# Products of three fp32r matmuls on split operands become one plain fp32 matmul

## Chip, cores and metric

The program runs on one core of one Trainium2 chip. The metric is the device time of one execution in microseconds (us). Tensors are fp32 in memory.

## What is computed

Two blocks over 256 latent tokens ("x") and 256 context tokens, of width 1024, each of two layers. Cut to what matters:

```python
# first block, per layer l (context tokens only where a later layer needs them)
hx = rms_norm(x, norm1_g[l]) * (1.0 + sc1) + sh1
y_lat, y_ctx = token_mixers(hx, hc, w_in[l], w_out[l], ...)  # gating, Fourier, two attentions
x = x + g1 * y_lat
x = x + g2 * expert_choice_ffn(rms_norm(x, norm2_g[l]) * (1.0 + sc2) + sh2,
                               router_w[l], exp_w_gate[l], exp_w_up[l], exp_w_down[l])
# second block, per layer i
h = h + 0.5 * swiglu(rms_norm_2(h, ffn1_norm[i]), ffn1_w_gate[i], ffn1_w_up[i], ffn1_w_down[i])
h = h + m          # layer 0: rglru_mixer (recurrence), layer 1: pool_mixer
h = h + 0.5 * swiglu(rms_norm_2(h, ffn2_norm[i]), ffn2_w_gate[i], ffn2_w_up[i], ffn2_w_down[i])
gate = jax.nn.sigmoid(rms_norm_2(h, ple_norm[i]) @ ple_w_gate[i])
h = h + gate * (p[i].astype(h.dtype) @ ple_w_proj[i])
```

`swiglu` is 1024 to 2816 and back, `rglru_mixer` projects 1024 to 2 x 1280 and 1280 back, and there are 16 experts of 1024 x 1024 per layer with 32 tokens each of a stream. The modulation (`sh`, `sc`, `g`) comes from `ada_w`.

## The kernel before

Activations lie with features on partitions; a product takes a 128x128 tile of a weight or of the activations as the stationary operand and 256 or 512 columns as the moving one. SP streams all weights in chunks of 128 x 4096 floats (2 MB) into `ring`, which has six slots, in the order of use; before the load of a chunk SP waits on `weights_used`, which PE raises as it finishes chunks. Each engine has its program written out by hand, stage by stage, with semaphores between them.

Except in the experts, the modulation (`ada_group`), the attentions and a few small ones, a product is `exact` (L691): operands are split into a lead, which is the value rounded to fp32r, and the rest, value minus lead; three fp32r matmuls add lead x lead, lead x rest and rest x lead:

```python
release(pe.matmul(out, a[0], b[0], start=start, stop=False, skip_group_check=True))
pe.matmul(out, a[0], b[1], start=False, stop=False, skip_group_check=True)
return pe.matmul(out, a[1], b[0], start=False, stop=stop, skip_group_check=True)
```

Weights are split once per chunk: ACT copies it to a second slot as fp32r (`halve_lead`, L348 to L354), DVE writes the rest over the original (`halve_rest`, L356 to L361). Such a chunk takes two of the six slots. The calls for it are put by hand into ACT's and DVE's programs between the work of the stages. Activations are split likewise: after the norm into the mixers (L610 to L645), for the feed-forward blocks (`norm_squares_lead` L594 on ACT, `norm_rest` L647 on DVE), for the merged heads (L1419 and L1865), for the feed-forward's hidden values (L1476, L2002), and for the recurrence's output (L1525, L2097). The token rows that the one-hot gather (L978) reads are split as well, and the rows of affinities and slots that are spread over partitions (L990).

A norm whose gain is applied before the product leaves its factor 1/std to be multiplied in when PSUM is read; its mean comes from eight fp32 matmuls against `mean_w` (`norm_pe`, L567), which stand ahead of a feed-forward block's first product. A feed-forward block (`ffn_group`, L1046) works in groups of four feature tiles: gate and up products to PSUM banks 0 to 3, then the down products, which sum in banks 4 to 7 over all groups; `open_sums` (L1091) clears these. Its first 16 tiles and the experts run in hardware loops (`Fori`). `add_sums` (L2024) adds the sums to the residual `x_res`. The expert products (L1011, L1026) are plain fp32. Their chunks take one slot each, six chunks to an expert. `scatter_back` (L1042) returns the experts' results to tokens. Other lines named below: L833, L846 and L855 are attention with difference, L871, L885 and L900 local attention, L1135 the recurrence's gates, L1188 the pooling's map, L723 and L731 the modulation.

Of the kernel before, what the change touches and what calls it, by code (L numbers as in the profile page):

```python
# [16 lines left out]
F32 = mybir.dt.float32  # L17
F32R = mybir.dt.float32r
# [59 lines left out]
def lru_pairs():  # L78
# [20 lines left out]
    "y_squares": 4, "y_sums": 4, "y_std": 4, "y_normed": 4, "y_turned": 8, "y_t": 8, "y_rest": 8, "mix_out": 8, "mix_added": 8,  # L99
    "logits": 1, "logits_copied": 1, "logits_turned": 1, "logits_shifted": 1, "logits_exp": 1,  # L100
    "h_turned": 8, "h_tok_lead": 8, "h_tok_rest": 8,
    "aff": 1, "aff_turned": 1, "slots": 1, "slots_turned": 1, "spread_rows": 2, "spread": 2, "aff_copied": 2,
# [24 lines left out]
def build(nc, dram, out_t):  # L127
    ctx = ExitStack()
    with ctx:
# [12 lines left out]
        def large(stack, suffix, dt):  # L142
            return [stack.enter_context(nc.sbuf_tensor(name + suffix, shape, dt)) for name, shape in (
                ("ring", [P, SLOTS, SLOT]), ("h_buf", [P, KT, 2 * N]), ("arena", [P, 16384]))]

        with ExitStack() as first:
            ring, h_buf, arena = large(first, "", F32)
        ring_r, h_buf_r, arena_r = large(ctx, "_r", F32R)
# [17 lines left out]
        expand = sb("expand", [64, 4 * P], F32R)  # L166
# [26 lines left out]
        in_lead, out_lead = h_buf_r, h_buf_r  # L193
        in_exact = part(0, 4096).rearrange("p (k t) -> p k t", k=KT)
        in_rest, out_rest = (arena_r[:, a:a + 4096].rearrange("p (k t) -> p k t", k=KT) for a in (0, 4096))

# [8 lines left out]
        h_flat_r = h_buf_r[:, :, :].rearrange("p k t -> p (k t)")  # L205
        spread_rows = h_flat_r[:, 3072:4096].rearrange("p (s w t) -> p s w t", s=2, w=2)
        aff_bc = part(8192, 9216).rearrange("p (g t) -> p g t", g=4)
        expand_in = part(8192, 8704)[0:64, :]

        h_tok = arena_r[:, 8192:12288].rearrange("p (t f) -> p t f", t=4)  # L210
        h_tok_rest = [a.rearrange("p (t f) -> p t f", t=4) for a in (arena_r[:, 12288:14336], h_flat_r[:, 0:2048])]
# [3 lines left out]
        gather = arena_r[:, 14336:16384].rearrange("p (t e s) -> p t e s", t=4, e=EXPERTS)  # L215
# [4 lines left out]
        h_lead, h_rest = h_buf_r[:, :, 0:N], h_buf_r[:, :, N:2 * N]  # L220
# [4 lines left out]
        hid_lead, hid_rest = (arena_r[:, a:a + 1024].rearrange("p (f t) -> p f t", f=4) for a in (512, 1536))  # L225
# [7 lines left out]
        y_lead, y_rest = (arena_r[:, a:a + RT * N].rearrange("p (o t) -> p o t", o=RT) for a in (12880, 2560))  # L233
# [32 lines left out]
        for l in range(LAYERS):  # L266
            norms += [(2 * N, 2, False), (2 * N, 2, True) if l == 0 else (N, 1, True)]
        norms += [(N, 1, False)] * (4 * LAYERS + 1)

        def in_halves(i):  # L270


            return i >= 2 * LAYERS and i not in (POOL_NORM, LAST_NORM)

        scaled_before = [sum(KT * s for j, (_, s, _) in enumerate(norms[:i]) if not in_halves(j))
# [11 lines left out]
        loads, halved = [], []  # L287

        def stream(key, *chunks):
            chunk_at[key] = len(loads)  # L290
            for dmas, floats in chunks:
                loads.append(dmas)
                halved.append(floats)

        PLAIN, HALVED = (1, 0), (1, SLOT)
        for l in range(LAYERS):
            if l == 0:
                stream(("ada", 0), *[PLAIN] * 4)
            stream(("w_in", l), HALVED, HALVED, HALVED, (2, SLOT), (1, KT * GROUP))
            if l == 0:  # L300
                for step in range(1, 5):
                    stream(("ada", step), *[PLAIN] * 4)
            stream(("w_out", l), HALVED, HALVED)
            if l == 0:
                stream(("ada", 5), *[PLAIN] * 4)
            stream(("experts", l), *[PLAIN] * 6 * EXPERTS)
# [2047 lines left out]
```

## Time and profile before

| | us |
|---|---|
| median of 3 runs (all: 2717.77, 2713.36, 2715.48) | 2715.48 |
| span of the profiled execution, first to last instruction | 2717.3 |
| mean granted TensorE clock over the span | 0.965 |
| instructions in the span | 32508 |
| HBM read | 657.71 MB |

The runs' times come without a split into span and surroundings; the profiled span lies inside the range of the runs. In the profile, PE is TensorE's matmuls, PEld its weight loads, DVE is VectorE, ACT ScalarE, POOL GpSimd, SP the engine that issues the weights' transfers. "L694" is line 694 of the kernel. Matmuls are pipelined: the duration of one is longer than the distance from its start to the next. A share of the clock of 1.00 is the upper level, 2.4 GHz, 0.5 is 1.2 GHz.

The span's stages by time: up to 48 us the first loads and the modulation; to 396 the mixers of layer 0 and its routing; to 898 gather, experts; to 1158 the mixers and routing of layer 1, to 1648 its experts; then the second block, in which four feed-forward blocks begin at 1670, 1994, 2234 and 2470, with the recurrence at 1865 and the embedding stages at 2189 and after 2660.

### The profile page before, as it was taken

To read this page: it belongs to the slowest core of one execution; us is meant where nothing else is said; L and a number is where in the kernel's file an instruction comes from. 1 tells how busy PE (TensorE), PEld (TensorE's weight loads), DVE (VectorE), ACT (ScalarE), POOL (GpSimd) and SP (SyncE) were. 2 spreads that over 40 slices of the span, in tenths; PEclk is the share of its full clock that TensorE was granted. 3 is DMA by queue.
4 is the path that set the end of the run, shared out by engine and by line. 5 is a ranking of instruction groups with operands and counts; after the bars stand their busy time and mean duration, and the time that the engine had idled before them with its cause. 6 is when DMAs were issued, how large, how long until landed. Compare 5 with 4: busy or idle time off the path is not lost.

```text
span 2717.3 us, 32508 instructions
## 1 busy us (share of the span) xinstructions
PE 2302.9 (85%) x13952; PEld 1613.8 (59%) x13952; DVE 1037.0 (38%) x1361; ACT 811.7 (30%) x989; POOL 67.6 (2%) x99
## 2 busy tenths in 40 slices
PE   5998888777777898787777778999999989988997
PEld 3855643222222585631111116999899989988997
DVE  4536451000000455510000004556855555556555
ACT  3425321000000344410000004432744354434433
POOL 0022000000000002000000000000000000000000
PEclk8999899999999998899999999999999999999998
DMA  7392357999999330389999995554355444452542
GB/s 264 109 385 107 120 220 280 409 409 410 410 410 410 143 131 6 118 323 409 409 410 410 410 410 204 179 180 175 123 186 186 167 149 165 181 186 93 186 165 72
DMA packets 205376, 660.17 MB, mean 243 GB/s; under 512 B 5632, under 2 KB 27136, under 8 KB 198624
## 3 DMA queue, kind: packets, MB, share of 16 engines
q1 hardware_dynamic: 204176, 653.67, 62.6%
q0 software_dynamic: 1104, 5.11, 0.5%
q8 instruction: 73, 1.20, 0.2%
q14 instruction: 23, 0.19, 0.0%
HBM read 657.71 MB, written 1.05 MB: 242 GB/s over the span
## 4 chain that ended last, share of the span: by engine, by line
PE 57%; DMA 29%; DVE 7%; ACT 4%; SPq 2%; issue 1%; POOL 0%; DVEq 0%; ACTq 0%; POOLq 0%
PE ps L694 13%; PE ps L695 13%; PE ps L696 13%; DMA ring<-in_exp_up 13%; DMA ring<-in_exp_gate 11%; PE ps L1011 6%; DMA ring<-in_w_in 2%; DVE ring_r L361 2%; PE ps L567 2%; SPq L453 2%; DMA ring<-in_ffn_gate 2%; ACT ring_r L354 1%; PE ps L833 1%; PE ps L1026 1%; PE ps L723 1%
## 5 line engine op out<-in xcount | busy, mean ns | idle before, releaser
L1011 PE MATMUL ps<-ring,arena 128*64 128x512 f32 (+1 forms) x2048 | 466.6, 600 | 165.1 <-DMA ring<-in_exp_up 81.9
L694 PE MATMUL ps<-h_buf_r,ring_r 128*128 128x256 f32 (+1 forms) x1856 | 540.8, 291 | 17.6 <-DVE h_buf_r L652 12.2
L696 PE MATMUL ps<-h_buf_r,ring_r 128*128 128x256 f32 (+1 forms) x1856 | 537.9, 290 | 0.0
L361 DVE TENSOR_TENSOR ring_r<-ring,ring_r 128x4096 fp32r<-128x4096 f32 (+2 forms) x97 | 406.2, 4192 | 304.6 <-ACT ring_r L354 304.6
L695 PE MATMUL ps<-h_buf_r,ring_r 128*128 128x256 f32 x1696 | 482.9, 285 | 0.0
L1011 PEld LDWEIGHTS ps<-ring,arena 128*64 128x64 f32 (+1 forms) x2048 | 128.2, 124 | 502.2 <-issue 295.3
L354 ACT ACTIVATE ring_r<-ring 128x4096 fp32r<-128x4096 f32 (+2 forms) x97 | 332.7, 3434 | 262.4 <-DMA ring<-in_ffn_down 107.6
L694 PEld LDWEIGHTS ps<-h_buf_r,ring_r 128*128 128x128 f32 x1856 | 360.4, 194 | 22.9 <-issue 16.7
L696 PEld LDWEIGHTS ps<-h_buf_r,ring_r 128*128 128x128 f32 x1856 | 360.2, 194 | 3.3
L695 PEld LDWEIGHTS ps<-h_buf_r,ring_r 128*128 128x128 f32 x1696 | 328.8, 194 | 0.2
L695 PE MATMUL ps<-arena_r,ring_r 128*128 128x256 f32 (+1 forms) x944 | 278.3, 295 | 0.0
L1026 PE MATMUL ps<-ring,arena 128*64 128x512 f32 (+1 forms) x1024 | 232.1, 596 | 45.4 <-DMA ring<-in_exp_down 25.6
L1968 DVE TENSOR_TENSOR arena<-arena,ps 128x512 f32<-128x512 f32 (+1 forms) x32 | 21.9, 683 | 588.1 <-PE ps L1011 588.1
L694 PE MATMUL ps<-arena_r,ring_r 128*128 128x256 f32 x784 | 223.3, 285 | 3.4 <-DVE arena_r L2002 1.8
L696 PE MATMUL ps<-arena_r,ring_r 128*128 128x256 f32 x784 | 222.7, 284 | 0.0
L695 PEld LDWEIGHTS ps<-arena_r,ring_r 128*128 128x128 f32 x944 | 183.1, 194 | 3.3
L1026 PEld LDWEIGHTS ps<-ring,arena 128*64 128x64 f32 (+1 forms) x1024 | 61.8, 123 | 194.7 <-issue 118.3
L694 PEld LDWEIGHTS ps<-arena_r,ring_r 128*128 128x128 f32 x784 | 151.4, 193 | 4.5 <-DVE arena_r L2002 2.1
L696 PEld LDWEIGHTS ps<-arena_r,ring_r 128*128 128x128 f32 x784 | 151.4, 193 | 0.0
L1976 DVE COPY arena<-ps 32x512 f32 x32 | 22.0, 686 | 299.0 <-PE ps L1026 299.0
L1458 ACT ACTIVATE arena<-ps 128x512 f32<-128x512 f32 (+1 forms) x32 | 15.7, 490 | 340.0 <-PE ps L1018 340.0
L694 PE MATMUL ps<-ring_r,h_buf_r 128*128 128x512 f32 (+1 forms) x240 | 92.0, 384 | 16.4 <-DVE arena_r L633 16.4
(273 smaller groups left out, 2325.0 us busy)
## 6 DMA issues: line engine op xcount, KB each, us to landing
ring<-in_exp_gate SPq DMA_DIRECT2D x64, 2048.0 KB, 23.7
ring<-in_exp_up SPq DMA_DIRECT2D x64, 2048.0 KB, 23.8
ring<-in_exp_down SPq DMA_DIRECT2D x64, 2048.0 KB, 23.7
ring<-in_ada_w SPq DMA_DIRECT2D x24, 2048.0 KB, 14.7
ring<-in_ffn_gate SPq DMA_DIRECT2D x20, 2048.0 KB, 7.7
ring<-in_ffn_up SPq DMA_DIRECT2D x20, 2048.0 KB, 7.8
ring<-in_ffn_down SPq DMA_DIRECT2D x20, 2048.0 KB, 7.9
ring<-in_w_in SPq DMA_DIRECT2D x6, 2048.0 KB, 20.8
```

Of the source, the lines that this page charges most:

```text
L354: act.activation(halves(n)[0][:, 0:halved[n]], slot(n)[:, 0:halved[n]], ACT.Copy).then_inc(sem("chunk_lead"), 1)
L361: dve.tensor_tensor(rest, slot(n)[:, 0:halved[n]], lead, ALU.subtract).then_inc(sem("chunk_halved"), 1)
L453: sp.dma_start(slot(n + c).rearrange("p (k n) -> p k n", k=4), src)\
L567: mm = pe.matmul(ps[:, 0, 0:width], mean_w[:, :], squares(i)[:, k, 0:width], start=k == 0, stop=k == KT - 1)
L694: release(pe.matmul(out, a[0], b[0], start=start, stop=False, skip_group_check=True))
L695: pe.matmul(out, a[0], b[1], start=False, stop=False, skip_group_check=True)
L696: return pe.matmul(out, a[1], b[0], start=False, stop=stop, skip_group_check=True)
L723: mm = pe.matmul(ps[32 * j:32 * j + 32, 7, :], cond[:, k, :], slot(n + k // 2)[:, at:at + 512], start=k == 0, stop=k == KT - 1)
L833: pe.matmul(ps[:, 2 * (u % 3) + m, 0:width], q_band[:, 2 * (u % 4) + m, :], qk_t[:, 2 + (2 * h + m) // 4, lo:lo + width], start=True, stop ...
L1011: mm = pe.matmul(ps[half * m:half * m + m, which, :], xe[:, k, :], slot(n + c)[:, D * (k % 4) + 512 * half:D * (k % 4) + 512 * half + 512] ...
L1026: mm = pe.matmul(ps[half * m:half * m + m, 3, :], hid_t[:, k % 4, k // 4, :], slot(n + c)[:, D * (k % 4) + 512 * half:D * (k % 4) + 512 * ...
L1976: ins = dve.tensor_copy(o[32 * j:32 * j + 32, it, 512:1024], ps[m + 32 * s:m + 32 * s + 32, 3, :])
```

## The change

Every `exact` product is one plain fp32 matmul on unsplit operands. All lead and rest buffers, the two splitting functions and their calls on ACT and DVE are gone, and with them the fp32r views of the memory. Each chunk takes one ring slot, so SP may run six chunks ahead everywhere. The `Fori` loops are written out. Moved with it: for the feed-forward blocks ACT writes the gained tile first and the squares after (`norm_gained`), and `norm_pe` comes behind the third tile of gate products, `open_sums` behind the first; the merged heads are transposed into eight banks and read alternately by ACT and DVE, as are the token rows for the gather; the projections of the merge and of the embedding use eight banks instead of six; the spreading matmul has 16 rows and reads affinities and slots where they lie. What the experts compute, and their matmuls, stay as they were.

```diff
-            def exact(out, a, b, start, stop):
...
-                release(pe.matmul(out, a[0], b[0], start=start, stop=False, skip_group_check=True))
-                pe.matmul(out, a[0], b[1], start=False, stop=False, skip_group_check=True)
-                return pe.matmul(out, a[1], b[0], start=False, stop=stop, skip_group_check=True)
...
-            stream(("w_in", l), HALVED, HALVED, HALVED, (2, SLOT), (1, KT * GROUP))
+            stream(("w_in", l), 1, 1, 1, 2, 1)
...
+        slot_of = [n % SLOTS for n in range(len(loads))]
+        slot_free = [max(0, n - SLOTS + 1) for n in range(len(loads))]
...
-        def norm_squares_lead(act, i, gain, added):
+        def norm_gained(act, i, gain, added):
+
+            name, start, tiles = added
             for k in range(KT):
+                if k % tiles == 0:
+                    act.wait_ge(sem(name), start + k // tiles + 1)
+                act.activation(h_buf[:, k, 0:N], x_res[:, k, 0:N], ACT.Copy, scale=gain(k)).then_inc(sem("norm_gained"), 1)
             for k in range(0, KT, 2):
-                act.wait_ge(sem(name), start + (k + 1) // tiles + 1)
                 act.activation(squares(i)[:, k:k + 2, :], x_res[:, k:k + 2, 0:N], ACT.Square).then_inc(sem("norm_squares"), 2)
-                for j in (k, k + 1):
-                    act.activation(h_lead[:, j, :], x_res[:, j, 0:N], ACT.Copy, scale=gain(j)).then_inc(sem("norm_led"), 1)
...
                     for f in range(tiles):
-                        if which and f == size:
+                        if step == 0 and which == 0 and f == 1:
+                            open_sums()
+                        if step == 0 and which == 0 and f == 3:
+                            norm_pe(pe, release, norm)
+                        if step == 0 and which and f == size:
                             pe.wait_ge(sem("norm_std"), norm + 1)
...
-                            mm = exact(ps[:, bank, lo:lo + N], half_cols(w, at, at + P),
-                                       h_tile(k), k == 0, k == KT - 1)
+                            mm = pe.matmul(ps[:, bank, lo:lo + N], slot(c)[:, at:at + P], h_buf[:, k, 0:N],
+                                           start=k == 0, stop=k == KT - 1)
...
-                        for i, h in enumerate((h_tok[:, 2 * s + a, P * k:P * k + P],
-                                               h_tok_rest[k // 4][:, 2 * s + a, at:at + P])):
-                            mm = pe.matmul(ps[:, j % 6, :], h, one_hot, start=a == 0 and i == 0, stop=a == 1 and i == 1)
+                        mm = pe.matmul(ps[:, j % 6, :], h_tok[:, 2 * s + a, P * k:P * k + P], one_hot, start=a == 0, stop=a == 1)
```

On PE, the start of the first feed-forward block, behind the scatter-back of layer 1 (first row); each row is a run of matmuls with output, operands and moving shape. Before, where the block's products begin a loop (the branch row):

```order
L1042 MATMUL ps<-arena 128x256 x32
L567 MATMUL ps<-arena,mean_w 128x256 x8
L1091 MATMUL ps<-zeros 128x512 x4
L1096 UNCONDITIONAL_BRANCH
L1096 ISA
L694 MATMUL ps<-h_buf_r,ring_r 128x256
L695 MATMUL ps<-h_buf_r,ring_r 128x256
L696 MATMUL ps<-h_buf_r,ring_r 128x256
L694 MATMUL ps<-h_buf_r,ring_r 128x256
```

and in the changed kernel (L944 is the scatter-back, L970 gate and up products, L998 `open_sums`, L513 `norm_pe`, L984 down products):

```order
L944 MATMUL ps<-arena 128x256 x32
L970 MATMUL ps<-h_buf,ring 128x256 x8
L998 MATMUL ps<-zeros 128x512 x4
L970 MATMUL ps<-h_buf,ring 128x256 x16
L513 MATMUL ps<-arena,mean_w 128x256 x8
L970 MATMUL ps<-h_buf,ring 128x256 x40
L984 MATMUL ps<-arena,ring 128x256 x32
```

The eight norm matmuls now stand behind 24 products instead of ahead of them, and a product is one row of one line.

On DVE, from the end of the first feed-forward block to the recurrence (L2002 is the last rest of the hidden values, L2024 the adds to the residual, L652 the rest of the normed tiles, L2056 the first read of the recurrence). Before:

```order
L2002 TENSOR_TENSOR arena_r<-arena,arena_r 128x256
L361 TENSOR_TENSOR ring_r<-ring,ring_r 128x4096
L2024 SCALAR_TENSOR_TENSOR x_res<-ps,x_res 128x2x256 x4
L652 SCALAR_TENSOR_TENSOR h_buf_r<-x_res,vec,h_buf_r 128x256 x8
L655 RECIPROCAL arena<-arena 128x256
L2049 MEMSET arena 128x10x3
L361 TENSOR_TENSOR ring_r<-ring,ring_r 128x4096
L361 TENSOR_TENSOR ring_r<-ring,ring_r 128x2048
L2056 TENSOR_TENSOR arena<-ps,arena 128x256
L2058 TENSOR_SCALAR arena<-arena,vec 128x256
L2061 SCALAR_TENSOR_TENSOR arena<-arena,vec 128x256 x3
```

and in the changed kernel (L1842 the last hidden values, L1851 the adds, L560 the reciprocal of the norm, L1880 the first read):

```order
L1838 TENSOR_TENSOR arena<-ps,arena 128x256
L1842 TENSOR_TENSOR arena<-arena 128x256
L1851 SCALAR_TENSOR_TENSOR x_res<-ps,x_res 128x2x256 x4
L560 RECIPROCAL arena<-arena 128x256
L1876 MEMSET arena 128x10x3
L1880 TENSOR_TENSOR arena<-ps,arena 128x256
L1882 TENSOR_SCALAR arena<-arena,vec 128x256
L1885 SCALAR_TENSOR_TENSOR arena<-arena,vec 128x256 x3
```

The adds follow the hidden values with nothing in between, and none of the three splits of a chunk is left.

## Rows read from the trace of the kernel before

**Rows 1.** The page: busy time by engine, share of the span, instructions.

```profile
PE 2302.9 (85%) x13952; PEld 1613.8 (59%) x13952; DVE 1037.0 (38%) x1361; ACT 811.7 (30%) x989; POOL 67.6 (2%) x99
```

**Rows 2.** Windows: us, busy us (instructions) of PE, PEld, DVE, ACT, POOL; PE clock, DMA share, GB/s.

```profile
461.00:881.00 420.00, 311.76 (x1384) 96.08 (x1384) 33.69 (x56) 37.00 (x59) 0.00 (x0) 1.00 1.03 410
...
1672.00:1857.00 185.00, 185.00 (x1544) 185.00 (x1543) 98.18 (x64) 76.58 (x44) 0.00 (x0) 1.00 0.47 165
...
1865.00:1960.00 95.00, 90.69 (x623) 86.29 (x624) 79.48 (x143) 54.33 (x90) 0.00 (x0) 0.96 0.44 158
```

**Rows 3.** Groups by line and form: busy us, mean ns; idle before, its releasers.

```profile
L694 PE MATMUL ps<-h_buf_r,ring_r 128*128 128x256 f32 x1776 | 508.8, 286 | 15.4 <-DVE h_buf_r L652 12.2 <-DVE ring_r L361 2.0 <-DVE arena_r L1865 1.2
...
L694 PE MATMUL ps<-arena_r,ring_r 128*128 128x256 f32 x784 | 223.3, 285 | 3.4 <-DVE arena_r L2002 1.8 <-DVE arena_r L2097 1.6
...
L694 PE MATMUL ps<-ring_r,h_buf_r 128*128 128x512 f32 x208 | 83.0, 399 | 16.4 <-DVE arena_r L633 16.4
...
L694 PE MATMUL ps<-h_buf_r,ring_r 128*128 128x512 f32 x80 | 32.0, 400 | 2.2 <-DVE arena_r L1865 2.2
...
L694 PE MATMUL ps<-ring_r 128*128 128x256 f32 x32 | 9.1, 283 | 0.0
...
L694 PE MATMUL ps<-ring_r,h_buf_r 128*128 128x256 f32 x32 | 9.0, 283 | 0.0
...
L978 PE MATMUL ps<-arena_r 128*128 128x512 f32 x72 | 24.0, 450 | 4.8 <-DVE arena_r L1925 4.8
...
L978 PE MATMUL ps<-arena_r,h_buf_r 128*128 128x512 f32 x24 | 9.3, 389 | 0.0
...
L990 PE MATMUL ps<-h_buf_r,expand 64*128 64x512 f32 x12 | 4.4, 493 | 4.7 <-DVE arena L1947 2.9 <-DVE arena L1941 1.8
...
L567 PE MATMUL ps<-arena,mean_w 128*128 128x256 f32 x160 | 43.2, 423 | 13.5 <-ACT arena L599 8.7 <-ACT arena L580 4.8
...
L885 PE MATMUL ps<-const,arena 128*128 128x128 f32 x80 | 14.9, 306 | 14.0 <-ACT arena L1373 14.0
...
L1042 PE MATMUL ps<-arena 128*128 128x256 f32 x128 | 31.3, 397 | 5.4 <-DVE x_res L1876 2.7 <-DVE h_buf L1976 1.7 <-DVE arena L1976 1.0
```

**Rows 4.** PE timeline, split products 512 columns wide: start us, us, instruction.

```profile
75.00 0.39 PE L694 MATMUL ps<-ring_r,h_buf_r 128*128 128x512 f32 x1
...
79.53 0.39 PE L696 MATMUL ps<-ring_r,arena_r 128*128 128x512 f32 x1
```

**Rows 5.** PE timeline, plain fp32 products 256 columns wide.

```profile
915.89 1.89 PE L1042 MATMUL ps<-arena 128*128 128x256 f32 x8
917.62 1.67 PE L1042 MATMUL ps<-arena,h_buf 128*128 128x256 f32 x7
```

**Rows 6.** Chain that ended last, in order of time: start us, us, piece.

```profile
1022.47 5.17 PE ps L833 x12
...
1899.68 22.61 PE ps L1135 x104
```

**Rows 7.** DVE and PE timelines at the first products of layer 0; [idle before <- releaser].

```profile
38.91 0.17 DVE L1662 SCALAR_TENSOR_TENSOR gain<-mod,vec 128x16 f32<-128x16 f32 x1
42.69 4.42 DVE L361 TENSOR_TENSOR ring_r<-ring,ring_r 128x4096 fp32r<-128x4096 f32 x1 [3.61 <-ACT ring_r L354]
...
48.78 0.77 PE L694 MATMUL ps<-ring_r,h_buf_r 128*128 128x512 f32 x1 [10.40 <-DVE arena_r L633]
```

**Rows 8.** DVE timeline from the first feed-forward block to the recurrence.

```profile
1858.06 4.42 DVE L361 TENSOR_TENSOR ring_r<-ring,ring_r 128x4096 fp32r<-128x4096 f32 x1
1862.39 2.48 DVE L2024 SCALAR_TENSOR_TENSOR x_res<-ps,x_res 128x512 f32<-128x512 f32 x4
```

**Rows 9.** PE timeline: first products after hand-overs, with the idle time before.

```profile
1865.41 0.36 PE L694 MATMUL ps<-h_buf_r,ring_r 128*128 128x256 f32 x1 [4.09 <-DVE h_buf_r L652]
...
2228.21 5.28 PE L567 MATMUL ps<-arena,mean_w 128*128 128x256 f32 x16 [4.60 <-ACT arena L599]
```

More of the change, by code:

```diff
@@ L138, in sem @@
             return sems[name]
[L142 to L148, printed above, removed]
+        ring = sb("ring", [P, SLOTS, SLOT])
+        h_buf = sb("h_buf", [P, KT, 2 * N])
+        arena = sb("arena", [P, 16384])
         x_res = sb("x_res", [P, KT, 2 * N])
@@ L566, in norm_pe @@
                 pe.wait_ge(sem("norm_squares"), KT * i + k + 1)
-                mm = pe.matmul(ps[:, 0, 0:width], mean_w[:, :], squares(i)[:, k, 0:width], start=k == 0, stop=k == KT - 1)
+                mm = pe.matmul(ps[:, mean_bank(i), 0:width], mean_w[:, :], squares(i)[:, k, 0:width], start=k == 0, stop=k == KT - 1)
                 if k == 0:
@@ L1021, in experts @@
+                for e in range(EXPERTS):
+                    xe = x_exp[:, 512 * (e % 2):512 * (e % 2) + KT * m].rearrange("p (k m) -> p k m", k=KT)
+                    pe.wait_ge(sem("x_exp"), e + 1 + before("x_exp", l))
+                    for which in range(2):
                         for k in range(KT):
-                            c = 6 * j + 4 + k // 4
+                            c = n + 6 * e + 2 * which + k // 4
                             if k % 4 == 0:
-                                pe.wait_ge(slot_loaded[slot_of[n + c]], it * 64 + (loaded_value(n + c)))
+                                chunk(c)
@@ L1030, in experts @@
                                 mm.then_inc(weights_used, 1)
+                    pe.wait_ge(sem("exp_hid"), e + 1 + before("exp_hid", l))
+                    for b in range(4):
+                        mm = pe.transpose(ps[:, 2, P * b:P * b + P], hid_exp[:, P * b:P * b + P], ident)
+                    mm.then_inc(sem("exp_turned"), 1)
+                    pe.wait_ge(sem("exp_hid_t"), e + 1 + before("exp_hid_t", l))
+                    for k in range(KT):
+                        c = n + 6 * e + 4 + k // 4
+                        if k % 4 == 0:
+                            chunk(c)
+                        for half in range(2):
+                            mm = pe.matmul(ps[half * m:half * m + m, 3, :], hid_t[:, k % 4, k // 4, :],
+                                           slot(c)[:, D * (k % 4) + 512 * half:D * (k % 4) + 512 * half + 512],
+                                           start=k == 0, stop=k == KT - 1)
+                        if k % 4 == 3:
+                            mm.then_inc(weights_used, 1)
             def scatter_back(l):
@@ L1427, in route @@
                     .then_inc(sem("logits_copied"), 1)
-                for j in range(2 * tiles):
+                for j in range(0, 2 * tiles, 2):
                     half, t = divmod(j, tiles)
@@ L1493, in lru, with ffn @@
+            def ffn(i):
+                for g, tiles in enumerate(GROUPS):
+                    size = tiles // 2
+                    for b in range(2):
+                        act.wait_ge(sem("ffn_gate_scaled"), FFN_BANKS * i + 2 * g + b + 1)
+                        gates = silu_f[:, size * b:size * b + size, :]
+                        act.activation(gates, gates, ACT.Silu).then_inc(sem("ffn_silu"), 1)
             def lru():
                 v = lambda name: vec2[:, columns(VEC2, name)]
-                n = chunk_at["lru", 0]
```

595 lines of the change are left out of this document (194 added, 401 removed).

## The prediction

> **What bounds the kernel now.** I read the page first, then the windows, then the groups by form, then the timelines.
>
> The page has PE busy 85% of the span [rows 1]. Windows divide that into two regimes [rows 2]. In the expert stages (420 us shown here, and about as long again in layer 1) the DMA share is 1.03 at 410 GB/s while PE is busy 312 of 420 us: the weights' arrival sets the pace. Everywhere else PE does. In the first feed-forward block the window of 185.00 us has 185.00 us of PE, 1544 matmul records, the upper clock level (1.00) and a DMA share of only 0.47. 185.00 / 1544 gives 0.120 us per record. The "286 ns" of the groups [rows 3] is a pipelined duration, not a spacing; the sum must use spacings.
>
> So a product costs three spacings now: 3 x 0.120 = 0.360 us at 256 columns. At 512 columns twenty records take 79.53 - 75.00 = 4.53 us [rows 4], so 3 x 0.2265 = 0.680 us.
>
> A plain fp32 product leaves two records here. By the program L1042 issues 96 products (8 x 4 for each of three streams), and it has 192 records; L1135 issues 52 and has 104. Eight records of L1042 take 917.62 - 915.89 = 1.73 us [rows 5], 0.216 each, so 0.432 us per product of 256 columns; the 104 records of L1135 take 22.61 us [rows 6], 0.435 per product, with the last one's drain in it. At 512 columns twelve records take 5.17 us [rows 6], 0.431 each, 0.862 per product. These are 128x128 weights that change with each product, from ring and arena, as in the changed code. **Three split matmuls are thus cheaper than one plain one**: 0.360 against 0.432, and 0.680 against 0.862.
>
> A page of the Trainium skill speaks of this, "FP8 and Floating Point Precision", section Matmul Precision: true fp32 takes four passes, reduced-precision fp32 one. If each pass cost what a split matmul does, a product would be 0.480 us; the plain rows here say 0.432, so the measurement decides against that literal reading, which is a rival below.
>
> **The matmul term.** The groups of L694 count the products [rows 3]: 1776 + 784 + 32 + 32 = 2624 of 256 columns, 208 + 80 = 288 of 512.
> - 2624 x 0.072 = +188.9 us. Of it 2112 products, +152 us, are the four feed-forward blocks.
> - 288 x 0.182 = +52.4 us, in the input and output projections.
> - Gather: 72 + 24 = 96 records now at about 0.2265 (21.8 us); after, 48 products x 0.862 = 41.4: +19.6 us. It stands before the experts, whose ring holds only one expert's six chunks, so a later start is not made up.
> - Spread: 12 records, one per product; 12 x (0.862 - 0.24) = +7.5 us, also before the experts. The 0.24 is an estimate from the 512 spacing.
>
> All of this lies in PE-paced stretches, so it counts in full: +268.4 us. Expert products were plain fp32 already; their stages keep their length and only start later. Unrolling the loops costs nothing in my sum: the feed-forward window has no gap at the loops' turns, the expert stage's cover is the saturated DMA, and the matmul instructions to be fetched become fewer. If fetching did show, it would be as PE idle inside an expert, up to the 108 us in 420 that PE is idle there anyway [rows 2].
>
> **What goes away.** The split of a chunk costs ACT about 3.6 us and DVE 4.4 us [rows 7]. Most lie beside PE's work and are worth nothing; those in front of a waiting PE are worth what PE idles.
> - Idle before L694 in all forms is 15.4 + 3.4 + 16.4 + 2.2 = 37.4 us [rows 3]. At the start PE waits 10.40 us while ACT and DVE split the first chunk (DVE from 42.69 to 47.1) [rows 7]; without it one scaling and one shift, about 1 us, follow the gains at 39.1, worth 8.5 us. From feed-forward to recurrence the adds of the sums stand behind a 4.42 us split on DVE [rows 8] and PE waits 4.09 us [rows 9]; now each pair is added as its sum ends, ACT scales the early tiles while PE still works on the last, and PE should hardly stop. Two more hand-overs, to the embedding stage, are alike. I take 30 of the 37.4 us; what is late next is ACT's shift after the adaptive norm, and the gelu at the end of the recurrence.
> - The normalisation's matmuls L567 at 256 columns wait 13.5 us [rows 3], 4.60 at one place [rows 9], and there their 16 records take 5.28 us where 16 x 0.216 is 3.5. They now stand behind three tiles of products, their squares ready. -6 for the waits, -6 for the slow pace over several places.
> - In local attention L885 waits 14.0 us [rows 3]; the output projection's first chunk is split on ACT and DVE in mid-pipeline, once per layer. -8 us.
> - Scatter-back L1042 waits 5.4 us [rows 3], mostly for an add behind a split: -3. Merge and routing lose one subtraction per tile on DVE in chains that PE waits for, an estimated -5.
> - Every such stop is followed by low clock. The window from 1865 to 1960 has 0.96 [rows 2], that is 8% of 95 us at the lower level, some 4 us of work lost; fewer stops over the last 1050 us give back an estimated 10.
>
> Sum: -30 - 12 - 8 - 8 - 10 = -68 us. DVE's new work (scaling half of the transposed tiles) replaces a longer one. The deeper ring (a slot per chunk instead of two) adds no speed while DMA is at 0.47; it removes one late chunk, about 2 us, which I count in the 30.
>
> 2717.3 + 268.4 - 68 = 2917.7 us of span. The median of the runs is 1.8 us below the profiled span, so **about 2917 us**, 7.4% slower.
>
> Bounds. The matmul term goes from 262 (gather and spread as far hidden as the start of the experts could allow) to 275 (0.435 per product). The gains go from 0 to about 95 (all 37.4, 13.5, 14.0 and 5.4 us, 15 of clock and 10 of pace). The ends are 2717 + 262 - 95 = 2884 and 2717 + 275 - 0 = 2992; I take the range to where the gains are at least 30.
>
> **Rivals.**
> - *The stops stay.* Where a split stood, another link of the chain (table loads, the reciprocal, the wait for the last add) keeps PE waiting. For it: idle by several releasers overlaps, and longer products make the clock's low stretches dearer. Against it: the split stands alone ahead of PE at the two places that I looked up [rows 7, 8]. 2717 + 268 = 2985 us. Chance 0.07.
> - *Four full passes.* The page's rule at this kernel's own spacing: 4 x 0.120 = 0.480, as a mechanism the weight path limiting each pass as it does for the split matmuls. 2624 x 0.120 + 288 x 0.226 + about 30 = 410; 2717 + 410 - 68 = 3059 us. The plain products speak against it [rows 5, 6]. Chance 0.03.
> - *Weight loads are the bound (the other side: faster).* PEld is busy 185.00 of 185.00 us [rows 2], so the 0.120 us spacing may be that of the loads: at 512 columns it is only 0.2265, less than twice as long. If a plain product were limited by its loads alone, it would be two loads, 0.240 us instead of 0.360: -315 us, and 288 x -0.227 = -65 at 512 columns; 2717 - 380 - 68 = 2269 us. It wins from the point where a 256-column plain record is spaced under 0.180 us. L1042 and L1135 show 0.216 with weight loads of the same shape, so 0.02.
> - That the change leaves some splitting in place is excluded by the listing of the order: each run of three lines is one line, and no rounding copy of the ring is left.
>
> **Chances.** The forecast has 0.86, the stops staying 0.07, four passes 0.03, faster 0.02, anything else 0.02. The range 2885 to 2960 holds the main case with gains from 30 to 95 us. A measurement of this kernel can tell about 0.2% from no change. Faster has the loads' case, 0.02; the same 0.01; slower the rest.
>
> **What would show it.** Right: the feed-forward products at 0.432 us each in two records, each block about 228 us instead of 190; DVE's share far lower, with no operation on the ring at all; PE idle before the first product of the recurrence and the embedding stages under 1 us; the expert stages of the same length at 1.03 DMA share; the first product at about 40 us instead of 48.8. Wrong: a spacing per record other than 0.216, a clock under 0.95 inside a feed-forward block, or PE gaps of several us where the splits were.

## The result and the profile after

The changed kernel takes 2907.24 us (median of 4 runs, 2905.01 to 2908.2), the kernel before 2716.06 beside it (2713.36 to 2717.77). The ratio is 1.0701 with a 95% interval of [1.0686, 1.0716]: **slower by 7.0%**, as forecast (2917 us, 2885 to 2960), 10 us under the number given. Measured once more it took 2909.75 us, ratio 1.0710 [1.0696, 1.0725].

The page of the changed kernel, in the columns of [rows 1]:

```profile
PE 2540.9 (87%) x11047; PEld 1595.9 (55%) x11052; DVE 557.1 (19%) x1091; ACT 420.7 (14%) x802; POOL 67.7 (2%) x99
```

DVE and ACT are busy for about half of what they were, and the time rose: what their work gave back is less than what the dearer products cost. PE idles 365.5 us (2906.4 less 2540.9) where it idled 414.4 (2717.3 less 2302.9). Windows of the changed kernel, columns as in [rows 2]: the experts of layer 0, the whole last stretch from the second scatter-back to the end, and 185 us inside the second feed-forward block:

```profile
455.00:931.50 476.50, 361.76 (x1600) 113.54 (x1600) 38.17 (x63) 37.89 (x64) 0.00 (x0) 0.99 1.01 403
1705.50:2906.40 1200.90, 1168.94 (x5383) 1024.26 (x5388) 220.38 (x388) 134.41 (x259) 9.96 (x11) 0.99 0.40 141
2090.00:2275.00 185.00, 185.00 (x859) 162.86 (x858) 20.24 (x28) 8.05 (x12) 0.00 (x0) 1.00 0.40 141
```

and the same two stages of the kernel before:

```profile
421.80:897.80 476.00, 360.75 (x1600) 111.92 (x1601) 38.43 (x63) 41.73 (x67) 0.00 (x0) 1.00 1.01 403
...
1648.50:2717.30 1068.80, 1008.85 (x7900) 987.56 (x7900) 615.78 (x585) 462.11 (x412) 9.96 (x11) 0.97 0.45 158
```

The expert stage is as long as it was (476.5 against 476.0 us) and only starts later; the last stretch grew by 132.1 us. That stretch holds 2512 products of 256 columns (L970 1408, L984 704, recurrence 240, embedding 160). 2512 x 0.072 is 180.9 us, so 49 us were won back in it. In the feed-forward window 185.00 / 859 is 0.215 us per record, as in [rows 5]. The chain of waits shows the same in pieces (start us, us, piece):

```profile
1765.31 27.63 PE ps L970 x128
1792.94 13.81 PE ps L984 x64
1806.75 27.63 PE ps L970 x128
1834.38 13.81 PE ps L984 x64
```

27.63 / 128 = 0.216 per record, two records per product, **0.432 us per product** with no gap between the pieces. Groups by form of the changed kernel (columns as in [rows 3]):

```profile
L970 PE MATMUL ps<-h_buf,ring 128*128 128x256 f32 x2816 | 613.2, 379 | 3.8 <-ACT h_buf L545 3.8
L984 PE MATMUL ps<-arena,ring 128*128 128x256 f32 x1408 | 307.8, 379 | 0.0
...
L662 PE MATMUL ps<-ring,h_buf 128*128 128x512 f32 x288 | 127.4, 604 | 6.1 <-ACT h_buf L537 3.9 <-DMA ring<-in_w_in 2.1
...
L513 PE MATMUL ps<-arena,mean_w 128*128 128x256 f32 x160 | 36.2, 379 | 2.1 <-ACT arena L526 2.1
...
L1077 PE MATMUL ps<-arena,ring 128*128 128x256 f32 x160 | 34.8, 379 | 0.6 <-DVE arena L1915 0.6
...
L944 PE MATMUL ps<-arena 128*128 128x256 f32 x128 | 29.2, 380 | 2.5 <-DVE h_buf L1820 1.6 <-DVE arena L1820 0.9
...
L893 PE MATMUL ps<-h_buf,expand 16*128 16x512 f32 x24 | 16.5, 848 | 4.6 <-DVE arena L1792 2.8 <-DVE arena L1786 1.7
...
L694 PE MATMUL ps<-arena,h_buf 128*128 128x256 f32 x48 | 13.5, 450 | 3.9 <-DMA h_buf<-in_att 3.9
...
L789 PE MATMUL ps<-const,arena 128*128 128x128 f32 x80 | 13.3, 281 | 6.2 <-ACT arena L1282 6.2
```

Against [rows 3]: the idle time before the products fell from 37.4 to 10.5 us (3.8 + 6.1 + 0.6, the others have none), the norm's (L513, before L567) from 13.5 to 2.1, local attention's (L789, before L885) from 14.0 to 6.2, the scatter-back's (L944, before L1042) from 5.4 to 2.5. The norm's 160 matmuls now take 379 ns each and not 423. L694 is here the Fourier mixer; its 3.9 us of waiting for the load of a table are new.

What gather and spread cost can be read from the chain, first a piece of each before (L978, L990), then the same pieces now (L882, L893):

```profile
395.36 16.28 PE ps L978 x64
...
416.57 2.06 PE ps L990 x4
```

```profile
405.68 29.41 PE ps L882 x64
...
444.44 7.21 PE ps L893 x8
```

All pieces together, the gather took 25.9 us and takes 44.9, the spread took 4.4 and takes 16.6: **31 us more**, where 27.1 were booked. The gather was priced right (19.0 against 19.6); the spread costs 12.2 and not 7.5, since part of it runs at the lower clock level: the eight records shown take 7.21 us (granted clock 0.57 from 435 to 452 us), eight in layer 1 take 3.68.

### The profile page after: what moved, and what is told of

Same layout as the page of the kernel before. It is cut to its first block, busy times and chain, and to the rows that moved or that the text cites. A ratio compares the mean times of both kernels' runs of the same rounds, so it can differ in the third digit from the quotient of the medians.

```text
span 2906.4 us, 24937 instructions
## 1 busy us (share of the span) xinstructions
PE 2540.9 (87%) x11047; PEld 1595.9 (55%) x11052; DVE 557.1 (19%) x1091; ACT 420.7 (14%) x802; POOL 67.7 (2%) x99
## 4 chain that ended last, share of the span: by engine, by line
PE 67%; DMA 26%; DVE 4%; ACT 2%; SPq 1%; issue 1%; POOL 0%; DVEq 0%; ACTq 0%; POOLq 0%
PE ps L970 21%; DMA ring<-in_exp_up 18%; PE ps L984 10%; PE ps L913 5%; DMA ring<-in_exp_gate 5%; PE ps L662 5%; PE ps L828 3%; PE ps L1118 2%; PE ps L659 2%; PE ps L513 2%; DMA ring<-in_exp_down 2%; PE ps L882 2%; PE ps L944 1%; PE ps L625 1%; PE ps L1077 1%; PE ps L1061 1%
## 5 line engine op out<-in xcount | busy, mean ns | idle before, releaser
L970 PE MATMUL ps<-h_buf,ring 128*128 128x256 f32 x2816 | 613.2, 379 | 3.8 <-ACT h_buf L545 3.8
L970 PEld LDWEIGHTS ps<-h_buf,ring 128*128 128x128 f32 x2816 | 534.9, 190 | 77.6 <-issue 4.6
L984 PE MATMUL ps<-arena,ring 128*128 128x256 f32 x1408 | 307.8, 379 | 0.0
L984 PEld LDWEIGHTS ps<-arena,ring 128*128 128x128 f32 x1408 | 267.5, 190 | 36.4
L662 PE MATMUL ps<-ring,h_buf 128*128 128x512 f32 (+1 forms) x352 | 140.9, 563 | 6.1 <-ACT h_buf L537 3.9
L1833 DVE TENSOR_TENSOR arena<-ps,arena 128x512 f32<-128x512 f32 (+1 forms) x48 | 31.1, 647 | 485.8 <-PE ps L970 485.7
L662 PEld LDWEIGHTS ps<-ring,h_buf 128*128 128x128 f32 x352 | 68.0, 194 | 78.4 <-issue 71.1
L828 PE MATMUL ps<-h_buf,ring 128*128 128x512 f32 (+1 forms) x256 | 83.5, 488 | 0.0
L1838 DVE TENSOR_TENSOR arena<-ps,arena 128x512 f32<-128x512 f32 (+1 forms) x48 | 31.1, 647 | 256.5 <-PE ps L970 256.5
L513 PE MATMUL ps<-arena,mean_w 128*128 128x256 f32 (+1 forms) x208 | 59.1, 438 | 16.2 <-ACT arena L526 16.2
L828 PEld LDWEIGHTS ps<-h_buf,ring 128*128 128x128 f32 x256 | 49.0, 192 | 33.6 <-issue 30.1
L513 PEld LDWEIGHTS ps<-arena,mean_w 128*128 128x128 f32 x208 | 40.0, 193 | 32.3 <-issue 27.2
```

The costliest lines, as they stand in the source:

```text
L513: mm = pe.matmul(ps[:, mean_bank(i), 0:width], mean_w[:, :], squares(i)[:, k, 0:width], start=k == 0, stop=k == KT - 1)
L662: mm = pe.matmul(ps[:, j % 6, 0:width], h, w[:, 512 * k + lo:512 * k + lo + width], start=k == 0, stop=k == KT - 1)
L828: mm = pe.matmul(ps[:, d, 0:width], slot(n)[:, at:at + P], h_buf[:, k, 0:width], start=k == 0, stop=k == KT - 1)
L970: mm = pe.matmul(ps[:, bank, lo:lo + N], slot(c)[:, at:at + P], h_buf[:, k, 0:N], start=k == 0, stop=k == KT - 1)
L984: mm = pe.matmul(ps[:, 4 + d // 2, N * (d % 2):N * (d % 2) + N], slot(c + 1)[:, at:at + P], hid_f[:, f, :], start=False, stop=False, skip_ ...
L1833: dve.tensor_tensor(silu_f[:, size * b:size * b + size, :], bank(1 + b), factors, ALU.mult).then_inc(sem("ffn_gate_scaled"), 1)
```

## The experiments

**Only the price of the product.** Of the change, this is the part that was thought to cost. The two products with the rests are left out; all splitting stays.

```diff
-release(pe.matmul(out, a[0], b[0], start=start, stop=False, ...))
-pe.matmul(out, a[0], b[1], start=False, stop=False, ...)
-return pe.matmul(out, a[1], b[0], start=False, stop=stop, ...)
+mm = pe.matmul(out, a[0].bitcast(F32), b[0].bitcast(F32), start=start, stop=stop, ...)
+release(mm)
+return mm
```

> The kernel before with one edit: a product is one plain fp32 matmul on the two leads (it leaves out the two products with the rests); all splitting, the two-slot chunks, the order and the loops stay. My theory: the matmul term alone, 2624 x 0.072 + 288 x 0.182 = 241 us plus part of the spread and gather (up to 27), on the 2716 of before: 2957 to 2984 us, so above the changed kernel's 2907 by 50 to 77 us, which is what the removed splits and the new order are worth. Rival 1, the splits went unseen and the price of a plain product was overstated: it comes out at the changed kernel's 2907 within 10 us. Rival 2, longer products cover the splits by themselves: the idle before the products' line falls from 37.4 us to under 20 and the time is below 2950.

Measured: 2927.07 us (2925.33 to 2931.73), ratio 1.0773 [1.0757, 1.0788]. That is 208.9 us over the 2718.22 beside it, where the price alone says 241; gather and spread are unaltered in this kernel. And it is 17 to 20 us over the changed kernel (2909.75 and 2907.24), where 50 to 77 were expected: the theory missed. Its page, its groups and its last stretch:

```profile
PE 2526.2 (86%) x11035; PEld 1596.8 (55%) x11040; DVE 1039.1 (35%) x1361; ACT 810.3 (28%) x989; POOL 67.7 (2%) x99
```

```profile
L694 PE MATMUL ps<-h_buf_r,ring_r 128*128 128x256 f32 x3552 | 778.5, 381 | 9.0 <-DVE h_buf_r L652 7.8 <-DVE arena_r L1865 1.2
L694 PE MATMUL ps<-arena_r,ring_r 128*128 128x256 f32 x1568 | 342.9, 379 | 3.1 <-DVE arena_r L2097 1.6 <-DVE arena_r L2002 1.5
...
L694 PE MATMUL ps<-ring_r,h_buf_r 128*128 128x512 f32 x416 | 184.3, 605 | 15.3 <-DVE arena_r L633 15.3
...
L694 PE MATMUL ps<-h_buf_r,ring_r 128*128 128x512 f32 x160 | 69.1, 593 | 2.3 <-DVE arena_r L1865 2.3
...
L567 PE MATMUL ps<-arena,mean_w 128*128 128x256 f32 x160 | 40.6, 409 | 8.2 <-ACT arena L599 4.3 <-ACT arena L580 3.8
```

```profile
1703.20:2927.50 1224.30, 1177.64 (x5383) 1027.20 (x5388) 617.80 (x585) 460.81 (x412) 9.96 (x11) 0.98 0.39 138
```

Splitting and order are untouched, and still the idle before the products fell from 37.4 to 29.7 us, the norm's from 13.5 to 8.2, and the granted clock of the last stretch rose from 0.97 to 0.98. The stretch grew by 155.5 us where the price says 180.9. So **32 us (241 less 209) were won back with every split still in place**. The page divides them. PE's idle time fell by 13 us (2927.5 less 2526.2 is 401.3, against 414.4), as much as the waits before the products and the norm lost: the same splits, adds and scalings of ACT and DVE hide better beside products that take longer. The other 18 or so lie inside PE's busy time, which grew by 223 us and not by 241. The clock fits as their cause: 0.972 of the upper level over the span, against 0.965, is an estimated 26 us less at the lower level (5.6% of 2927.5 against 7.0% of 2717.3), worth up to 13 us of work. No run altered the clock alone, so this part is not shown.

The second rival gave this time (below 2950), though not by its sign: it asked for under 20 us of idle, and 29.7 were left. The changed kernel must then have won some 50 us by all that this one lacks: the 17 to 20 between them and the 31 that gather and spread cost more there. That is the absent splits, the order, the new reading of heads and token rows, and the additional banks together.

**The order in the feed-forward blocks, partly put back.** In the changed kernel ACT writes eight gained tiles and then the squares, and the norm matmuls stand behind the third tile of products. Here:

```diff
-            for k in range(KT):
-                if k % tiles == 0:
-                    act.wait_ge(sem(name), start + k // tiles + 1)
-                act.activation(h_buf[:, k, 0:N], ... ACT.Copy, scale=gain(k)) ...
             for k in range(0, KT, 2):
+                act.wait_ge(sem(name), start + (k + 1) // tiles + 1)
                 act.activation(squares(i)[:, k:k + 2, :], ... ACT.Square) ...
+                for j in (k, k + 1):
+                    act.activation(h_buf[:, j, 0:N], ... ACT.Copy, scale=gain(j)) ...
...
                         if step == 0 and which == 0 and f == 1:
                             open_sums()
-                        if step == 0 and which == 0 and f == 3:
                             norm_pe(pe, release, norm)
```

> The changed kernel with the order of the normalisation in the feed-forward blocks partly put back: ACT squares and gains the tiles in alternation again, and PE runs the eight norm matmuls behind the first tile of products, not behind the third. My theory (order is worth 12 us with the norm ahead of all products): as PE now comes to them about 6.9 us earlier than in the changed kernel, 2 to 8 us slower, 2909 to 2915, with new idle before the norm's line or before the first products of a block. Rival, the order is worth nothing once the splits are gone: within 1 us of 2907.

Measured: 2916.95 us (2915.32 to 2917.82), ratio 1.0733 [1.0718, 1.0748]. Since the difference is not far above what two measurements of one kernel can differ by, both were measured once more, side by side.

> The changed kernel itself, unaltered, so that the runs with the norm early (2917) and with the old ring depth (2910) stand against it on one more chip. Theory: 2907 to 2909, the order of the norm worth 8 to 10 us and the ring depth 1 to 3. Rival: chips differ by as much as these differences, it comes at 2913 or more, and the two verdicts are open.

> The run with the norm early once more, on the same chip as the changed kernel. Theory: 8 to 10 us above it. Rival: under 4 us.

Measured there: 2909.75 us (2906.92 to 2911.66) for the changed kernel, 2915.32 (2913.6 to 2918.96) with the norm early. **The order is worth 6 us**, not 8 to 10. The first figure, 9.7, compared two kernels that had not run side by side. The PE timeline at the entry to the second feed-forward block shows the step. First of the changed kernel (start us, us, instruction, [idle before <- releaser]):

```profile
2083.49 3.62 PE L970 MATMUL ps<-h_buf,ring 128*128 128x256 f32 x16
2087.16 0.81 PE L998 MATMUL ps<-zeros 128*128 128x512 bf16 x3
2087.81 7.07 PE L970 MATMUL ps<-h_buf,ring 128*128 128x256 f32 x32
2094.71 3.62 PE L513 MATMUL ps<-arena,mean_w 128*128 128x256 f32 x16
```

then with the norm early (L968 is its product line):

```profile
2083.79 1.93 PE L968 MATMUL ps<-h_buf,ring 128*128 128x256 f32 x8
2085.91 1.13 PE L968 MATMUL ps<-h_buf,ring 128*128 128x256 f32 x4 [0.19 <-ACT h_buf L546]
2087.22 1.13 PE L968 MATMUL ps<-h_buf,ring 128*128 128x256 f32 x4 [0.19 <-ACT h_buf L546]
2088.41 0.81 PE L996 MATMUL ps<-zeros 128*128 128x512 bf16 x3
```

The first tile takes 4.62 us and not 3.67, because it waits for gained tiles with squares between them, in waits so short that the groups show only 5.4 us before L968 where the changed kernel has 3.8. If the other three blocks are like this one, four times 0.95 us give 3.8 of the 6; the rest is not located.

**The ring's run-ahead as it was.** SP's table `slot_free` is made as if each split chunk still took two slots; nothing else is altered.

```diff
-slot_free = [max(0, n - SLOTS + 1) for n in range(len(loads))]
+for n in range(len(loads)):
+    slots = [at % SLOTS, (at + 1) % SLOTS][:1 if n in plain else 2]
+    at += len(slots)
+    slot_free.append(max([0, n - SLOTS + 1] + [last_user.get(i, -1) + 1 for i in slots]))
+    last_user.update({i: n for i in slots})
```

> The changed kernel in which SyncE issues each weight load no earlier than the two-slot chunks of the kernel before would have let it. My theory (the deeper ring adds no speed, it removes one late chunk of about 2 us): 2907 to 2911 us. Rival, the run-ahead is a hidden part of the 79 us gained, as chunks stand ready when a stage begins: 2915 us or more, with idle of PE released by loads of the ring.

Measured: 2910.38 us (2906.5 to 2912.54), ratio 1.0707 [1.0692, 1.0723]; its interval overlaps that of the changed kernel, and 2909.75 is 0.6 us away. The last stretch is 1201.9 us against 1200.9. The deeper ring is worth nothing that these runs can tell.

**The order without the plain product.** The kernel before with its three matmuls, and of the change only the loops written out, the norm matmuls behind the third tile, the gained leads ahead of the squares; the second chunk is split ahead of the norm factor.

```diff
+            for k in range(KT):
+                if k % tiles == 0:
+                    act.wait_ge(sem(name), start + k // tiles + 1)
+                act.activation(h_lead[:, k, :], x_res[:, k, 0:N], ACT.Copy, scale=gain(k)) ...
...
+                        if step == 0 and which == 0 and f == 1:
+                            open_sums()
+                        if step == 0 and which == 0 and f == 3:
+                            norm_pe(pe, release, norm)
```

> The kernel before, with its three split matmuls kept, and of the change only what needs no plain product: feed-forward loops unrolled, the norm matmuls behind the third tile of products, all gained leads ahead of the squares, the second chunk's split ahead of the norm factor. My theory: of the 12 us credited to the norm, and a few of the hand-overs', 5 to 12 us come without the plain products: 2704 to 2711 us. Rival, those gains hang on the absent splits (ACT and DVE are then still busy with the ring's chunks and the squares come too late for the third tile): within 3 us of 2716, or slower.

Measured: 2712.85 us (2709.61 to 2713.76, 11 runs), ratio 0.998 [0.9971, 0.9989]. **It is the fastest kernel here that computes the whole, by 0.2% under the one before.** The gain of 5.4 us (beside 2718.22) is the low end of the 5 to 12 that were expected; the time itself lies just above the 2704 to 2711 written down. Its groups (L697 is the first of the three lines; nearly all the wait is in its first form):

```profile
L697 PE MATMUL ps<-h_buf_r,ring_r 128*128 128x256 f32 x1776 | 510.8, 288 | 24.2 <-DVE h_buf_r L653 23.1 <-DVE arena_r L1862 1.2
...
L567 PE MATMUL ps<-arena,mean_w 128*128 128x256 f32 x160 | 36.4, 380 | 3.3 <-ACT arena L580 3.3
```

The norm waits 3.3 us instead of 13.5, and its matmuls run 6.8 us shorter. But the products now wait 24.2 instead of 15.4, for the rests of the tiles: at the block's entry PE must have add, gained lead and rest, and what stood there before was the norm. So 17 us gone at the norm came back as 9 at the products.

**The loops alone.** The kernel before, with only the feed-forward blocks' `Fori` written out on PE, ACT and DVE.

```diff
-                with pe.Fori(0, FT // 8) as it:
-                    ffn_group(i, norm, n, it, 0, 4)
-                    ffn_group(i, norm, n + 3, it, 4, 4)
+                for g, tiles in enumerate(GROUPS):
+                    ffn_group(i, norm, n + 3 * g, None, 4 * g, tiles)
```

> The kernel before with only the feed-forward loops unrolled on PE, ACT and DVE. My theory: the turns of the loops cost nothing that PE waits for, 2716 us within 2. Rival, each turn's branch costs 2 us or more at 12 turns: 2692 us or less. If more instructions to fetch cost something, slower by over 3 us.

Measured: 2715.93 us (11 runs) beside 2717.27, ratio 0.9995 [0.9986, 1.0004]. No effect; the gain of the run before it is the order's. (The loops turn eight times on each engine, twice in each block, and not twelve times as the expectation has it; so its rival meant 2700 us or less, and is as far off.)

**Plain products with the order.** It joins the edits of the first run and of the reordered one.

> The kernel before with plain products (as in the run with plain products only: the two products with the rests are left out) and also the feed-forward order of the reordered run; all splitting stays. It divides the 47 us between the plain-only run and the changed kernel, once the dearer gather and spread (27 by the sum) are counted. Theory: the order is worth 5 to 10 us and the absent splitting the rest: 2927 less 5 to 10 is 2917 to 2922. Rival: order and longer products together already do what the absent splits were credited with, as each split is then covered: 2900 or less.

Measured: 2930.61 us (2926.56 to 2933.63), ratio 1.0781 [1.0767, 1.0794], against 1.0773 [1.0757, 1.0788] for plain products in the old order. Expected were 5 to 10 us less; there is no gain. Its groups:

```profile
L697 PE MATMUL ps<-h_buf_r,ring_r 128*128 128x256 f32 x3552 | 781.3, 382 | 16.6 <-DVE h_buf_r L653 15.5 <-DVE arena_r L1862 1.2
...
L567 PE MATMUL ps<-arena,mean_w 128*128 128x256 f32 x160 | 36.3, 380 | 3.8 <-ACT arena L580 3.8
```

With plain products the old order had left 8.2 us at the norm and 9.0 here. Moving the norm took 4.4 there and put 7.6 here: the wait is for the rest of the gained tile (L653), and the order cannot remove it. Only the absence of the rests does (3.8 us before the products in the changed kernel). Both theory and rival were wrong about the order's worth in this company.

**What sets the two spacings.** The gate and up products run on 128 and on 192 of the 256 columns, in the kernel before and in the changed one.

```diff
-mm = exact(ps[:, bank, lo:lo + N], half_cols(w, at, at + P), h_tile(k), ...)
+mm = exact(ps[:, bank, lo:lo + P], half_cols(w, at, at + P), tuple(t[:, 0:P] for t in h_tile(k)), ...)
```

> The kernel before with the gate and up products of the feed-forward blocks on the first 128 of 256 columns (half of the tokens is left out there, and stale sums are used). What sets the 0.120 us between two split matmuls of 256 columns? If the columns: 0.060 us per record. If the weight load of 128 x 128 that each matmul needs, or a mixture: 0.095 to 0.120, hardly less than now. My guess is the columns with a floor, 0.09.

> The changed kernel with the gate and up products on the first 128 of 256 columns (half of the tokens is left out there, and stale sums are used). The spacing of a plain record of 256 columns is 0.216 us. If the columns set it, 0.107 to 0.110 at 128, and the rival that weight loads bound a plain product is dead; if a load sets it, it stays over 0.15.

> The kernel before with the gate and up products on the first 192 of 256 columns (a quarter of the tokens is left out there). Split records were spaced 0.111 us at 128 columns and 0.120 at 256. If a floor of 0.111 (the weight load) holds up to where the columns pass it, 0.111 to 0.115 at 192, a product 0.333 to 0.345 us.

> The changed kernel with the gate and up products on the first 192 of 256 columns (a quarter of the tokens is left out there). Plain records were spaced 0.112 us at 128 columns and 0.216 at 256. If the columns set the spacing, 0.162 at 192, a product 0.324 us: then the plain product is the cheaper one at 192 columns, and the two cross between 192 and 256. Rival: the price steps up with a threshold and is 0.18 or more, and the split product stays cheaper.

Measured: 2694.97 us at 128 columns and 2682.03 at 192 with split products (one run each), 2622.79 and 2759.22 with plain ones. The spacings, first of split records 128 wide (PE timeline; the 192 records of a group's gate and up products begin with the first row and end with the second):

```profile
1703.08 0.22 PE L694 MATMUL ps<-h_buf_r,ring_r 128*128 128x128 f32 x1
...
1724.36 0.28 PE L696 MATMUL ps<-h_buf_r,ring_r 128*128 128x128 f32 x1
```

of those 192 wide, again 192 records:

```profile
1700.92 0.25 PE L694 MATMUL ps<-h_buf_r,ring_r 128*128 128x192 f32 x1
...
1722.23 0.27 PE L696 MATMUL ps<-h_buf_r,ring_r 128*128 128x192 f32 x1
```

of plain ones 128 wide and 192 wide (the chain of waits, one kernel each):

```profile
1755.42 14.29 PE ps L970 x128
```

```profile
1758.22 20.80 PE ps L970 x128
```

21.28 / 191 = 0.111 us and 21.31 / 191 = 0.112 us: a split record costs the same at 128 and at 192 columns, 0.120 at 256. Plain records take 14.29 / 128 = 0.112, 20.80 / 128 = 0.1625 and 0.216 us. So both kinds have a floor of 0.111 to 0.112 us at 128 columns. Fewer columns don't go below it by much, as local attention in the kernel before shows, with plain records 64 columns wide (PE timeline):

```profile
267.20 1.00 PE L900 MATMUL ps<-arena 128*128 128x64 f32 x8
268.05 0.65 PE L871 MATMUL ps<-arena 128*128 128x256 f32 x2
```

0.85 / 8 = 0.106 us each. Plain records have left it by 192 columns and grow with them; **split records stay on it up to 192 columns, and at 256 are 8% over it**. A product costs, split and plain: 0.334 and 0.223 us at 128 columns, 0.335 and 0.325 at 192, 0.360 and 0.432 at 256, 0.680 and 0.858 at 512. The last is from the changed kernel's chain:

```profile
122.70 27.47 PE ps L659 x64
```

27.47 / 64 = 0.429 per record. The two kinds cross between 192 and 256 columns, by an estimate a little above 192: for the narrow products the plain form would have been the faster one. The guess of 0.09 for 128 split columns was wrong, those for 192 columns right; for plain records of 128 columns 0.107 to 0.110 was expected, a little under the 0.112 measured.

These spacings also say what a plain product is. From 256 to 512 columns it gains 0.858 less 0.432 = 0.426 us and one split matmul 0.227 less 0.120 = 0.107: **four times as much per column**. The page of the Trainium skill that the prediction names ("FP8 and Floating Point Precision", Matmul Precision) gives true fp32 four passes, and in this slope the trace agrees; one pass for the reduced form is the prediction's own reading of it. The rival of 0.480 us failed because it took four times 0.120, and of that spacing a part is the floor and not the columns.

The split kernel was 13 us slower at 128 columns than at 192, and most of that is the clock. Windows inside the third feed-forward block, right behind the same stop of PE for a split, at 128 and then at 192 columns:

```profile
2230.50:2254.40 23.90, 23.89 (x112) 23.89 (x113) 10.07 (x10) 9.12 (x7) 0.00 (x0) 0.50 0.31 106
```

```profile
2228.70:2252.60 23.90, 23.84 (x206) 23.84 (x207) 15.08 (x12) 12.69 (x8) 0.00 (x0) 1.00 0.53 179
```

The first ran at the lower level, and PE did 112 records where the other did 206; some 11 us of work were lost in this one stretch. Why the clock fell behind the stop in one kernel and not in the other, these two runs do not tell.

The Trainium skill, "TensorE: Matmul & The Clock Gate", section LDWEIGHTS (loading the stationary operand), gives a load of 128 columns as 128 / 1.2 = 107 ns. The floor of 0.111 us lies 4% over that, and the load path of the split form is busy in all of its window [rows 2]. At the lower clock level the records of 128 columns are 23.89 / 112 = 0.213 us apart, so the floor goes with the clock, which the figure of the Trainium skill does not say. That the floor is the weight load fits all of this; no run here changed the width of a weight at few moving columns, so it is not shown.

## Why the prediction was right

- **The price of the product** was right in its parts: 0.216 us per record of 256 columns in the blocks, 0.432 per product. 1.00 of granted clock and no gap inside a block, as the forecast asked; a block's 528 products take 228 us. The 512-column product measured 0.858 where 0.862 was taken. The rival of four full passes (0.480) and that of the loads (faster, from under 0.180 per record) are both out. The first is wrong in its size, not in its count of four; the second is out for these widths only: at 128 columns it holds.
- **The stages** moved as said: experts of equal length, the first product at 38.61 us instead of 48.78, no ring operation on DVE.
- **The gains** were sized 68 us and came to about 79 (2717.3 + 268.4 - 2906.4, with the matmul term taken as summed; 83 with gather and spread as measured). Idle before products: 26.9 of the 30 taken. Norm: 11.4 of waiting where 6 were taken, and 7.0 of pace (43.2 to 36.2 busy) for 6. Local attention 7.8 for 8, scatter-back 2.9 for 3. These are 56 us; their waits, 49.0, are as much as PE's idle time lost (414.4 to 365.5). The other 23 (27 with gather and spread as measured) lie inside PE's busy time, where 15 were taken for the clock and for merge and routing. The clock fits here too: 0.965 and 0.977 over the span are an estimated 190 and 134 us at the lower level, and 56 us less of it are worth up to 28 us of work. This last part was not isolated. "Every such stop is followed by low clock" goes too far: the two windows behind the same stop, at 0.50 and at 1.00, show both.
- **That the total came within 10 us has some luck in it.** The spread was priced 4.7 us too low and the gain before the products 3.1 too high; against that stand 5.4 us more at the norm's waits and some 12 more for the clock and the rest. These errors partly cancel.
- **What the account does not see is the share of the dearer product in the gains.** The prediction booked the 68 us to what goes away, the splits, and to the norm's new place. As a sum for both changes together that is right in most items. But 32 us already come with the dearer product, with every split still there, and some 50 with the rest of the change, of which 6 are the order's. (The division depends on which step is taken first; splits cannot be taken out of the split form, so the other way round was not run.) The same order is worth 5 us beside split products and nothing beside plain ones with rests, since the wait moves from the norm to the first products. "-12 us for the norm" was under the 18 that came, and is no thing of its own: alone, the order mostly moved the wait.
- The check "PE idle before the first product of the recurrence and embedding stages under 1 us" held: L1022, L1061 and L1118 have 0.0. Of the two that it named as late next, ACT's shift after the adaptive norm is (L537, 3.9 us before L662); the gelu is not, as L1077 waits 0.6 us, for a product on DVE (L1915). The load of a table before the Fourier mixer (3.9 us) it did not name.
- The ring's depth and the loops were costed at 2 us and nothing; both are within what the runs tell from nothing.

Open: how the 50 us divide between the absent splits, the other edits and the clock.

## What to carry to other kernels

Price a change of precision by the spacing of records at the kernel's own width, since the two forms cross: here three split matmuls beat one fp32 matmul at 256 and 512 columns and lose at 128 and, by a little, at 192. When the bounding engine's work is made longer, subtract what comes back with it (here 32 of 241 us, about a seventh: 13 of idle time covered and 18 inside the busy time), before anything is credited to work removed from the engines beside it. A wait that is moved off one instruction must be looked for at the next: the reordered kernel took 17 us from the norm and kept 5.

## What was not expected of the hardware

The split record costs 0.111 us at 128 and 0.112 at 192 columns, 0.120 at 256 and 0.227 at 512: flat first, then 0.107 for the 256 columns from 256 to 512. The plain record reads 0.112, 0.1625, 0.216 and 0.429, and 0.106 at 64.

The experts' plain products, whose stationary operand is only 64 columns wide in layer 0 (chain of the kernel before), are half as dear at 512 columns:

```profile
446.95 13.76 PE ps L1011 x64
```

13.76 / 64 = 0.215 us per record, 0.430 per product, against 0.858 with 128 columns of weights. Whether that is the narrower operand, or that the two halves of an output go to different rows of PSUM, no run here tells.

A stretch of 24 us at the lower clock cost one kernel some 11 us at a place where its twin ran at the upper level. And two measurements of the same kernel differed by 2.5 us (2907.24 and 2909.75), with the kernel before differing by 1.7 beside them (2716.06 and 2717.77). That is as much as some of the effects asked for here; such effects need both kernels measured side by side.
